# The modulation weights in four chunks summed in PSUM, and x scaled and turned as it lands: the start of a hybrid attention layer

## What is computed

```python
mod = jax.nn.silu(c) @ w_ada + b_ada              # w_ada: 1024 x 3072
shift, scale, gate = jnp.split(mod, 3, axis=-1)
h = rms_norm(x, norm_pre) * (1.0 + scale[:, None]) + shift[:, None]
proj = h @ w_in                                   # w_in: 1024 x 11264
...                                               # window attention (6 stages), differential attention (4 stages)
y = rms_norm((ga * pa + gb * pb) @ w_out, norm_post)
return x + gate[:, None] * y
```

## Time and profile before

| | us |
|---|---|
| median of 3 runs (875.67 to 879.02) | 877.96 |
| the profiled execution's own time | 879.07 |
| its span, first to last instruction | 877.3 |
| TensorE busy | 818.3 (93%) |
| POOL / VectorE / ScalarE busy | 482.6 / 471.5 / 359.8 |
| mean granted TensorE clock | 0.982 |

### The profile page before, as it was taken

How to read it: one execution, slowest core, us unless ns; L and a number is a source line. 1 busy time by engine, 2 the same in 40 slices (tenths; PEclk the granted TensorE clock), 3 DMA queues, 4 the chain that set the end, 5 groups by cost and what they waited for, 6 DMA issues and landing times.

```text
span 877.3 us, 12629 instructions
## 1 busy us (share of the span) xinstructions
PE 818.3 (93%) x4622; PEld 687.9 (78%) x4622; DVE 471.5 (54%) x751; ACT 359.8 (41%) x774; POOL 482.6 (55%) x625
## 2 busy tenths in 40 slices
PE   1579799999999999999998999999899999999997
PEld 0468589788888888888877878778777777888897
DVE  2785678454454536323568669759756644102622
ACT  3334444344444344432444454454546542223410
POOL 2564655345655647245858359759645637736300
PEclk9979899999999999999998999999999999999999
DMA  9774284222333233324353133333121213333521
GB/s 251 198 217 105 67 285 121 86 73 86 96 121 94 80 117 97 97 72 137 105 138 96 49 110 97 109 97 86 57 88 49 60 37 117 99 97 106 182 97 49
DMA packets 92852, 94.87 MB, mean 108 GB/s; under 512 B 8269, under 2 KB 84086, under 8 KB 92662
## 3 DMA queue, kind: packets, MB, share of 16 engines
q1 hardware_dynamic: 92496, 93.64, 35.4%
q0 software_dynamic: 240, 0.39, 0.5%
q10 hardware_dynamic: 54, 0.02, 0.0%
HBM read 78.21 MB, written 5.34 MB: 95 GB/s over the span
## 4 chain that ended last, share of the span: by engine, by line
PE 69%; DVE 13%; issue 6%; DMA 4%; ACT 4%; SPq 2%; POOL 2%; DVEq 0%; POOLq 0%; ACTq 0%
PE proj L1502 50%; PE score L1381 4%; PE proj L1580 4%; PE sums L1427 3%; PE turned L1398 3%; DMA ada<-in_w_ada 2%; DVE dstat L1145 2%; PE score L1356 2%; ACT probs L891 2%; PE sums L1429 2%; DVE ada_sum L1025 1%; DVE dstat L1161 1%; DVE q_lo L1106 1%; DVE at_lo L1168 1%; ACT junk L923 1%
## 5 line engine op out<-in xcount | busy, mean ns | idle before, releaser
L694 POOL TENSOR_TENSOR w_lo<-raw,w_hi 128x256 fp32r<-128x256 f32 x392 | 316.4, 838 | 224.4 <-ACT w_hi L807 224.4
L1502 PE MATMUL proj<-h_hi,w_hi 128*128 128x512 f32 x608 | 253.3, 417 | 6.8 <-POOL h_lo L704 5.7
L1502 PE MATMUL proj<-h_hi,w_lo 128*128 128x512 f32 x608 | 241.8, 398 | 0.0
L1502 PE MATMUL proj<-h_lo,w_hi 128*128 128x512 f32 x608 | 241.0, 396 | 0.0
L1502 PEld LDWEIGHTS proj<-h_hi,w_hi 128*128 128x128 f32 x608 | 116.3, 191 | 42.1 <-issue 8.6
L1502 PEld LDWEIGHTS proj<-h_hi,w_lo 128*128 128x128 f32 x608 | 116.5, 192 | 26.6
L1502 PEld LDWEIGHTS proj<-h_lo,w_hi 128*128 128x128 f32 x608 | 116.7, 192 | 21.1
L807 ACT ACTIVATE w_hi<-raw 128x1024 fp32r<-128x1024 f32 x100 | 104.2, 1053 | 12.0 <-PE proj L1502 7.8
L719 POOL TENSOR_TENSOR rope_x<-rope_x,cos_t 128x512 f32<-128x512 f32 x36 | 55.9, 1552 | 69.5 <-DMA rope_s<-rope_x 69.5
L1168 DVE TENSOR_TENSOR at_lo<-turned,at_hi 128x512 fp32r<-128x512 f32 x64 | 43.9, 687 | 60.3 <-ACT at_hi L909 59.7
L891 ACT ACTIVATE probs<-score,dstat 128x512 f32<-128x512 f32 x64 | 43.4, 684 | 59.9 <-DVE dstat L1145 59.9
(11 more groups left out here) (245 smaller groups left out, 1522.1 us busy)
## 6 DMA issues: line engine op xcount, KB each, us to landing
raw<-in_w_in SPq DMA_DIRECT2D x88, 512.0 KB, 3.6
rope_s<-rope_x SPq DMA_DIRECT2D x144, 64.0 KB, 2.4
ada<-in_w_ada SPq DMA_DIRECT2D x16, 512.0 KB, 6.3
zd<-in_w_ada SPq DMA_DIRECT2D x8, 512.0 KB, 5.2
raw<-in_w_proj_b SPq DMA_DIRECT2D x8, 512.0 KB, 3.4
raw<-in_w_out SPq DMA_DIRECT2D x8, 512.0 KB, 4.1
rows_in<-window_rows SPq DMA_DIRECT2D x4, 792.0 KB, 4.9
window_rows<-rows_out SPq DMA_DIRECT2D x4, 528.0 KB, 4.9
```

What stands on the lines that cost most here:

```text
L694: ins = nc.gpsimd.tensor_tensor(lo[:, k, :], raw[:, n % RAW, k, :], hi.bitcast(F32)[:, k, :], ALU.subtract)
L1502: ins = mm(dst, left, right, start=k == 0 and n == 0, stop=k == nk - 1 and n == 2)
```

## The change

- `w_ada` comes in four chunks of 256 channels, each in eight transfers of 256 KB (one contraction row of 128 with shift and scale), each with a semaphore of its own, and each chunk in its own buffer. Chunks 1 to 3 are summed in the PSUM bank `turned`, one instruction of 128x512 for each contraction row; the last one writes to SBUF. Of chunk 0 three rows (`PE_ADA`) go through PE, and DVE sums five.
- x is loaded first, its power is made tile by tile, and a scaled tile is transposed at once into PSUM banks that are free then; slices 2 to 7 are kept in SBUF (`xt`, in `zd`).
- Each chunk gives two channel slices; PE makes the products of both for the four tiles, pass by pass over the tiles, and of the value tiles (two in a bank, in `score`) the first four slices. The other four follow at ticks 8 to 11. DVE makes six of the eight rests of h, POOL two.
- The first six halves have buffers of their own or are ordered slice by slice (`FIRST_LO`); block 3 is loaded with the first ones, into buffers of stage 1.
- Tiles 1 and 2 change places, so that q and k of the first two heads come first; their swap starts before the other two tiles are done, and the scores of these heads wait for this pair alone.
- The rotary tables are computed on a quarter of the columns (128 instead of 512, the four quarters on the partitions), stored to DRAM and loaded again in eight transfers.
- Positions and lambdas are loaded by SP, the latter late. The masks come ahead of the powers on POOL. `G_TICK` goes from 14 to 36.

```diff
@@ -114,6 +114,9 @@
     end = tick
     start_tick.append(end)
 
+    tiles[1], tiles[2] = tiles[2], tiles[1]
+    tiles[1].u, tiles[2].u = 1, 2
+
...
-    G_TICK = 14
+    G_TICK = 36
+    N_CH, PE_ADA = 4, (2, 5, 7)
+    DVE_ADA = [[kk for kk in range(KT) if ch or kk not in PE_ADA] for ch in range(N_CH)]
+    ADA_SUMS = [sum(len(p) for p in DVE_ADA[:ch + 1]) for ch in range(N_CH)]
     gate_row_at = by_tick(range(2), lambda i: G_TICK + KT + 1 + i)
...
-    for q in ((0, 0), (1, 0), (0, 1), (1, 1), (2, 0), (2, 1)):
+    for q in ((0, 0), (1, 0), (2, 0), (0, 1), (1, 1), (2, 1), (3, 0), (3, 1)):
         prep.setdefault(-1, []).append(q)
-    for b in range(3, NB):
...
+    FIRST_LO = ([(0, 0), (1, 0), (0, 1), (1, 1), (2, 0), (2, 1)], [(0, 2), (1, 2), (0, 3), (1, 3)], [(2, 2), (2, 3)],
+                [(3, 0), (4, 0), (3, 1), (4, 1), (3, 2), (4, 2), (3, 3), (4, 3)], [(5, k) for k in range(4)])
+    lo_count = {(halves[n], k): i + 1 for i, (n, k) in enumerate(q for part in FIRST_LO for q in part)}
+    lo_count.update({(q, k): 4 * n + k + 1 for q, n in block_no.items() if n >= 6 for k in range(4)})
...
+            ada_rows = w_ada[0].rearrange("(a p) (r n) -> p a r n", p=P, r=3)
+
+            def load_ada(ch, kk):
+                sp.dma_start(ada[ch][:, kk, :, :], ada_rows[:, kk, 0:2, ch * BW:(ch + 1) * BW]).then_inc(ada_loaded[ch][kk], 16)
...
+            sp.dma_start(rope_c[:], rope_rows).then_inc(pos_loaded, 16)
+            for q in range(NT):
+                sp.dma_start(pos[32 * q:32 * q + 32, :].bitcast(I32),
+                             positions[0, q * P:(q + 1) * P].partition_broadcast(32)).then_inc(pos_loaded, 16)
+            for kk in range(KT):
+                load_ada(0, kk)
+            for n in range(RAW):
+                load_half(n)
+            for kk in range(KT):
+                load_ada(1, kk)
+            for kk in range(KT):
+                load_ada(2, kk)
+            sp.wait_ge(mod_done, 1)
             load_half(3)
-            for k in range(4, KT):
-                load_ada(k)
+            load_half(4)
+            sp.wait_ge(x_turned, KT)
+            for kk in range(4):
+                load_ada(3, kk)
+            sp.wait_ge(act_sin, 3)
+            sp.dma_start(trig_rows.rearrange("q f a n -> (q f) a n"), trig).then_inc(trig_stored, 16)
+            for kk in range(4, KT):
+                load_ada(3, kk)
+            sp.wait_ge(trig_stored, 16)
+            for i in range(4):
+                for table, a in ((cos_t, 2), (sin_t, i % 2)):
+                    sp.dma_start(table[32 * i:32 * i + 32, :].rearrange("f (q n) -> f q n", q=NT),
+                                 trig_rows[:, :, a, :].rearrange("q f n -> f q n")).then_inc(trig_loaded, 16)
+            load_half(5)
+            for i, v in enumerate((lambda_q1, lambda_k1, lambda_q2, lambda_k2)):
+                sp.dma_start(lam_in[:, i, :], v[0].partition_broadcast(P)).then_inc(small_loaded, 16)
...
+                if n == 9:
+                    for pair in range(2):
+                        sp.wait_ge(rope_copied, 2 * pair + 2)
+                        for i in range(4):
+                            j = i ^ 1
+                            sp.dma_start(zd[32 * i:32 * i + 32, 4 + 2 * pair:6 + 2 * pair, :],
...
+            for tt in range(NT):
+                pool.wait_ge(act_x_sq, tt + 1)
+                link(nc.gpsimd.tensor_scalar(st[:, 4 + tt:5 + tt], st[:, tt:tt + 1], 1.0 / D, EPS, ALU.mult, ALU.add))
+                nc.gpsimd.tensor_tensor(st[:, 8 + tt:9 + tt], st[:, 4 + tt:5 + tt], half_c[:, 0:1], ALU.pow).then_inc(x_pow_done, 1)
...
+            for part in FIRST_LO[:2]:
+                for n, k in part:
+                    pool.wait_ge(w_hi_done, n + 1)
+                    cut_slice(n, k)
+            for k in (2, 3):
+                pool.wait_ge(h_hi_done, k + 1)
+                pool.wait_ge(h_f_done, k + 1)
+                nc.gpsimd.tensor_tensor(h_lo[:, k, :], h_f[:, k % 2, :], h_hi[:, k, :].bitcast(F32),
+                                        ALU.subtract).then_inc(h_lo_pool, 1)
+            for part in FIRST_LO[2:]:
+                for n, k in part:
+                    pool.wait_ge(w_hi_done, n + 1)
+                    cut_slice(n, k)
+            for half in prep_at(-1)[6:]:
...
+            keep_x(6)
+            keep_x(2)
+            keep_x(7)
+            keep_x(3)
+            cut_hi(halves[0])
+            h_round(0)
+            cut_hi(halves[1])
+            h_full(0)
+            h_round(1)
+            h_full(1)
+            cut_hi(halves[2])
+            act.wait_ge(angle_done, 1)
+            for a, sign in enumerate((-1.0, 1.0)):
+                nc.scalar.activation(trig[:, a, :], angle, ACT.Sin, scale=sign).then_inc(act_sin, 1)
+            act.wait_ge(angle_done, 2)
+            nc.scalar.activation(trig[:, 2, :], complement, ACT.Sin).then_inc(act_sin, 1)
+            for k in (2, 3):
+                h_round(k)
+                h_full(k)
+            cut_hi(halves[3])
+            cut_hi(halves[4])
+            for k in (4, 5):
+                h_round(k)
+                h_full(k)
+            cut_hi(halves[5])
+            for k in (6, 7):
+                h_round(k)
+                h_full(k)
...
+            def sum_ada(ch, kk):
+
+                dve.wait_ge(ada_loaded[ch][kk], 16)
+                kept = ada[ch][:, 0, :, :]
+                total = turned[:].rearrange("p (r n) -> p r n", r=2) if ch else kept
+                n = DVE_ADA[ch].index(kk)
+                if n == 0:
+                    if ch == 0:
+                        dve.wait_ge(silu_done, 1)
+                    elif ch == 1:
+                        dve.wait_ge(xt_act, 3)
+                    ins = ts_(total, kept, silu_c[:, 1, 0:1], None, ALU.mult)
+                else:
+                    dve.wait_ge(ada_used, ADA_SUMS[ch] - len(DVE_ADA[ch]) + n)
+                    ins = stt(out=kept if kk == DVE_ADA[ch][-1] else total, in0=ada[ch][:, kk, :, :],
+                              scalar=silu_c[:, 1, kk:kk + 1], in1=total, op0=ALU.mult, op1=ALU.add)
+                ins.then_inc(ada_used, 1)
+
+            def modulate(ch):
+
+                ks = slice(2 * ch, 2 * ch + 2)
+                at = lambda first: cols[:, first + 2 * ch:first + 2 * ch + 2]
+                dve.wait_ge(mod_done, ch + 1)
+                link(tt_(ab[:, 0, ks], sums[:, 4 * ch:4 * ch + 2], at(16), ALU.add))
+                link(stt(out=ab[:, 0, ks], in0=ab[:, 0, ks], scalar=1.0, in1=at(32), op0=ALU.add, op1=ALU.mult))
+                tt_(ab[:, 1, ks], sums[:, 4 * ch + 2:4 * ch + 4], at(8), ALU.add).then_inc(ab_done, 1)
...
+            for kk in DVE_ADA[0][:-1]:
+                sum_ada(0, kk)
+            for k in (4, 5):
+                dve.wait_ge(x_turned, k + 1)
+                nc.vector.tensor_copy(xt[:, k, :], turn_place(k)).then_inc(xt_dve, 1)
+            sum_ada(0, DVE_ADA[0][-1])
             dve.wait_ge(cols_done, 2)
...
+            modulate(0)
+            angles()
+            sum_ada(1, 0)
+            h_rest(0)
+            sum_ada(1, 1)
+            h_rest(1)
+            for kk in range(2, KT):
+                sum_ada(1, kk)
+            modulate(1)
+            for kk in range(KT):
+                sum_ada(2, kk)
+            modulate(2)
+            sum_ada(3, 0)
+            sum_ada(3, 1)
+            h_rest(4)
+            sum_ada(3, 2)
+            sum_ada(3, 3)
+            h_rest(5)
+            for kk in range(4, KT):
+                sum_ada(3, kk)
+            modulate(3)
+            h_rest(6)
+            h_rest(7)
...
-                if s.part == 0 and s.head == 0:
+                if s.stage == 0 and s.part == 0:
+                    pe.wait_ge(rope_lo_done, 2 if s.head < 2 else 4)
+                if s.part == 0 and s.head == 0 and s.stage:
...
+            def ada_piece(kk):
+
+                pe.wait_ge(ada_loaded[0][kk], 16)
+                for side in (1, 0):
+                    for k in range(2):
+                        mm(column(0, side, k), ada[0][:, kk, side, k * P:(k + 1) * P], silu_c[:, 1, kk:kk + 1],
+                           start=kk == PE_ADA[0] and side == 1 and k == 0, stop=False, skip_group_check=True)
+
+            def modulation(ch):
+
+                pe.wait_ge(ada_used, ADA_SUMS[ch])
+                if ch:
+                    pe.wait_ge(ab_done, ch)
+                for side in (1, 0):
+                    for k in range(2):
+                        ins = mm(column(ch, side, k), ada[ch][:, 0, side, k * P:(k + 1) * P], ones[:, 0:1],
+                                 start=ch > 0, stop=True, skip_group_check=True)
+                ins.then_inc(mod_done, 1)
...
+            for tt in range(NT):
+                if tt < 2:
+                    pe.wait_ge(x_norm_done, tt + 1)
+                else:
+                    pe.wait_ge(x_norm_act, tt - 1)
+                for k in range(6):
+                    x_turn(k, [tt])
+                if tt == 1:
```

(37 more changed lines are left out.)

362 lines of the change are left out of this document (187 added, 175 removed).

## The result

The changed kernel takes 863.38 us, the median of 4 runs (861.27 to 865.20), against 878.49 us of the kernel before on the same chip: a ratio of 0.985 (95% interval 0.982 to 0.988). Forecast was 847.6, with a range of 838 to 860. So the sign was right, half of the gain came, and the range missed. The profiled execution took 861.27 us, 859.4 of it span.

The account below looks back on a forecast made before the run. Behind the start, PE's own instructions bind; DVE's sums and the path to first scores hold the start. Profiled 877.3 - 30.4 (earlier scores) - 1.0 (clock) + 1.0 (gate row) = 846.9 span, 848.7 with 1.8 outside; median 847.6, range 838 to 860.

Parts of the forecast that it names:

- Data: Opening loads: 12.6 MB at 330 GB/s, last w_ada chunk in at 40 us (52 at 252 GB/s), so DVE is last.
- First product: PE's first product after x, transposes and chunk 0's modulation: at 21 us, 13 us earlier than before.
- The angles: Rotary angles on DVE, on a quarter of the columns, ahead of chunk 1's end: 2.5 us.
- The pitch of the sums: DVE's 512-column sums into PSUM: 0.68 us each, 5.5 us a chunk, undisturbed by POOL.
- PE's order: Behind each chunk's sums: four one-column matmuls of 0.27 us and three small instructions, with no wait for earlier PE products.
- The pair wait: First scores wait for one q/k pair only; the rope path, last by 4 us, releases them at 72 instead of 102.4.
- that rival: Shorter rope path: swap lands sooner, scores start at 66 to 68 us, time 841 to 844; chance 0.10.
- Behind the scores: After the first scores: 1.0 us gained from the clock and 1.0 lost to the moved gate row.
- The clock's 1.0 us: PE's slow clock after its idle stretch before the scores, about 2.3 us lost before: 1.0 counted gained (0 to 2.3).
- Its rival of 4 to 10 us: Gate row in its new place stalls PE over several ticks through DVE's 9 us wait: 851 to 857; chance 0.07.
- The rival of the late opening: Transfers at 252 GB/s or slowed DVE sums: last modulation at 54 to 56 us, time 856 to 858; chance 0.15.
- rival of a slow clock throughout: Small pieces with waits keep PE's whole opening at 1.2 GHz: 43 us more, 890; chance 0.04.

Follow-up runs that it names:

- SBUF version: Changed kernel with chunks 1 to 3 of w_ada summed in SBUF instead of the PSUM bank: 869.40 us, ratio 0.988.
- PE-order version: Changed kernel plus own-bank wait, block 4 cut at ticks 8/9, angles before first modulation, later chunks' sums earlier, chunk 2's modulation before value products: 852.51, again 853.75 us.
- own-bank version: Changed kernel, but the first scores wait only for the two value tiles of their own score bank, not all four: 865.20 us.

## Why the prediction missed

The sum put the span at 846.9; it was 859.4. Of the 12.5 us, 10.7 lie before the first scores (72.0 forecast, 82.7 measured), 1.8 behind them. The other 3.3 of the 15.8 are the step from the profiled execution to the median: I took off 1.1 us because the run of before was that much above its median, and this one was 2.1 below its own.

- **Data: right.** The last of `w_ada` was not last: 322 GB/s over the opening and 348 GB/s from 15 to 35 us, against 330 assumed. Transfers of 256 KB were no hindrance: the rule of the Trainium skill (DMA: Bandwidth & Descriptors, Measured) that the prediction weighed against them is not borne out in this trace, with many of them in the queue at once (one issued every 0.8 us, landing 7 to 8 us later).
- **First product: late by 2.7 us** (21 forecast, 23.7; 24.1 to 25.2 in the four other kernels with this program). PE stands until 13.8 us for the `w_ada` row of its second `ada_piece`, and the transposes of the last x tile stand behind it in program order (row below). It then ran them and the small matmuls at half its clock from 15 to 20 us, and the third `ada_piece` stands behind transposes that wait for ScalarE's copies.

```profile
13.82 1.05 PE L1694 MATMUL sums<-silu_c,ada 128*128 128x1 f32 x8 [0.49 <-DMA ada<-in_w_ada]
```

- **The angles: 4.4 us instead of 2.5.** I had scaled by their columns. Eleven short instructions, nearly all waiting for the one before, take 3.2 us even undisturbed, 0.22 us and more each; the other 1.2 are POOL's cuts beside three of them, a term that was put at nothing. Outside the chain they give every chunk 2.6 us back.
- **The pitch of the sums: the term that was mis-sized most.** I took 0.68 us, the duration of `at_lo`, and 5.5 us for a chunk. Where that row waits, it is for ScalarE and not for the DVE instruction before it; a sum is one of a chain, lasts 0.75 us and is followed after 0.86. Eight take 6.8 us, and three chunks 3.8 us more than the sum had. That POOL would not disturb them in PSUM was right, and the SBUF version shows what it would have cost otherwise, 6.9 us.
- **PE's order: the step that was left out.** I let each chunk's modulation follow its sums at once. In PE's program it stands behind value products, and DVE stood 4.6 us for it in three waits, 1.4 more than the sum had for the matmuls themselves; 1.2 of these are in chunk 2, whose sums end at 44.28 us and whose modulation PE starts at 45.44. With PE's modulation ahead of these products, and DVE's next sums ahead of its wait, the waits are 1.9 us in the PE-order version.
- These four make 2.7 + 1.9 + 3.8 + 1.4 = 9.8 of 10.5 us; the last modulation was known at 57.0 instead of 46.5 us. The rest lies in DVE's chain: 0.5 us ahead of the third sum of chunk 2 (bracket at 39.23), for which no cause is shown, and small items. From there to the end of the four tiles it took 9 us, 10 forecast.
- **The pair wait: worth 1.1 us, and the path was another.** The rope path from the end of the four tiles to `k_lo` of the second tile was 11.9 us and not 15.5: as short as that rival had it. It gained nothing, since the change adds a wait for all four value tiles in the same place, which the prediction put at nothing: 5.4 us of PE, among the second pair in DVE's order. The own-bank version shows that it was this wait, and that behind it stood another: 9.5 us of DVE for a swap that SP issues too late, passed on to PE as 3.3 us and a slow clock.
- **Behind the scores: +1.8, forecast 0.** The clock's 1.0 us wasn't gained: 7.3 us at 0.50 after the wait, 7.2 us at 0.57 before. The gate row cost PE 2.2 us of idle time in the profile, forecast 1.0; the medians do not show it. Its rival of 4 to 10 us did not come.
- **The rival of the late opening was the case**: the last modulation known at 54 to 56 us and a time of 856 to 858 were its terms, 57.0 and 863 came. Its price was about right and its chance (0.15) too small. I had tied it to slow data or slow sums, and it came from pitch, program order and a chain of short instructions. The forecast of 0.94 for faster was right. The clock as a whole did not turn against the change: 0.90 in the stretch of the products, and so the rival of a slow clock throughout did not come.
- **The range** reached the late opening, but with none of the new wait and none of the difference between one execution and the median. These two are 1.3 and 3.3 us and would have covered the result.

## What to carry to other kernels

Cost a chain of dependent instructions by its pitch in a row that is itself a chain, not by the duration of a lone one, and short links by their count as well as their width, each beside what the other engines do at that time. When a path is shortened, list every wait of the instruction at its end, the added ones too, and what each awaited engine has ahead of it in program order: here the gain went from a wait of PE to a wait of DVE to SP's queue to ScalarE's order before it reached the end. What an engine does in its idle time is free only in that place: the same angles cost 2.6 us inside the chain and next to nothing ahead of it. And before a profile of one version is held against another, compare their clocks behind the last wait: here it moved the same work by 1.4 to 1.7 us.

## What the runs showed of the hardware

- Two sums in a chain on DVE, each of 0.75 us in the trace, start 0.86 us apart; an instruction that does not wait for the sum before it starts 0.66 us after it. So the wait on the engine's own last result is worth 0.2 us, an estimate from these rows; no run takes the wait away.
- The contention of DVE's sums and POOL's cuts cost both engines: six sums 8.04 us instead of 5.05, two cuts 2.33 instead of 1.43. Narrow instructions suffer more in proportion: 0.23 us became 0.64 and 0.29 became 0.72 beside POOL.
- With six transfers, 0.39 MB in all, in a queue of POOL the DMA rate was 215 GB/s from 10 to 15 us; with these six through SP's queue, and 20 us later, it was 365.
- Waits of PE were followed by a stretch at half its clock of unequal length: 7.3 us at 0.50 after 5.4 us, 12 us at 0.58 after 3.3 us, and after the same wait of 3.8 us in the same program a clock of 0.89 or of 0.77 from 50 to 65 us. Where PE waits for DVE behind it the clock costs nothing (0.79 and 1.00 from 20 to 40 us, four tiles after 42.3 and 42.4 us). Behind the last such wait it costs: with 0.77 instead of 0.89 the tiles ended after 43.8 to 44.0.
